# Low parts of the first 18 weight tiles on VectorE inside the attention loop, the later ones on GpSimd in four pieces

## The chip, the cores and the metric

The kernel runs on one core of one Trainium2 chip. The metric is the device time of one execution in microseconds (us). Engines: TensorE (PE), VectorE (DVE), ScalarE (ACT), GpSimd (POOL) and SyncE (SP, which issues the loads).

## The reference

A causal decoder trunk of two layers over 512 tokens of width 1024, in float32, followed by a final RMSNorm:

```python
for layer in range(2):
    h = rms_norm(x, mix_norm_g[layer])
    y = even_mixer(h, ...) if layer == 0 else odd_mixer(h, ...)
    x = x + y
    x = x + conv_ffn(rms_norm(x, ffn_norm_g[layer]), ...)
return rms_norm(x, final_norm_g)
```

The even mixer has one input projection (1024 x 3072), rotary positions, four differential attention heads (A: two 64-wide maps and a 128-wide value each) and eight dilated heads of 64 (B), then an output projection. The odd mixer has multi-head latent attention (C, four heads) beside stick-breaking attention (D, four heads of 128), and an output projection. The MLP is `(silu(conv3(gate)) * value) @ w_down` with 2816 channels.

## The kernel before

**Three products for one.** The large matrix products are made from split operands. An operand `a` is rounded to a shorter format (`hi`), and the rest is `lo = a - hi`. TensorE then sums `h_hi*w_hi + h_hi*w_lo + h_lo*w_hi` (PASSES, L1064).

**Weight tiles.** All weights are cut into 101 tiles of 128 x 2048 float32 (1 MB), taken in a fixed order through two slots: tile n is in slot n % 2. For each tile, SyncE loads `w_raw` (L258), ScalarE rounds it to `w_hi` (split_hi, L356), GpSimd subtracts to get `w_lo` (split_lo, L276, one instruction over 2048 columns), and TensorE multiplies. The counters `w_hi_ready`, `w_lo_ready` and `mm_done` order this. SyncE loads tile n+2 only once `w_lo_ready` has counted tile n, since both hi and lo are made from the raw tile.

**Order in time.** Every engine has its own program, written out by hand, and they meet only at semaphores.

- Prologue, 0 to about 57 us: the first norm, token tile by token tile (square on ScalarE, L681 to L684 and L717 on VectorE, transposes on TensorE at L1072, high parts on ScalarE, low parts on VectorE at L699), woven with the projection of head group 0 from tiles 0 and 1 (L1371). VectorE copies the sums (L760) and does the rotary embedding of token tiles 2 and 3 itself (`rope`, L944 to L947); GpSimd does tiles 0 and 1 (rope_tile, L303 to L306).
- Head groups 0 to 6, in two loops (A: g = 0 to 3, B: g = 4 to 6), each with nine or ten steps k. At step k TensorE makes the scores of unit k (L1260 to L1264), then a part of the projection of the next group g+1 (part, L1226: parts 0 to 3 from tile 2g+2, parts 4 to 7 from tile 2g+3), the transposes of unit k-1 (L1287), and the value product of unit k-2 (L1305). VectorE makes the row maximum (L802), in B groups the multiplication with the dilation counts (L808, whose result the transposes wait for), the division of finished outputs (L815 to L826), and copies or adds each part (L767, L770). GpSimd, in its own loop, subtracts tile 2g+2, does the rotary embedding of the four token tiles as their parts come, and subtracts tile 2g+3. When all four are done TensorE transposes them (turn_qk, L1215) and the next group begins.
- Between A and B, VectorE makes the norm factors of the A outputs (L670, L690 to L692) and scales them (L974).
- Group 7 (B) has no next group. In its place the first half of the output projection is turned (L1171) and multiplied (L1191). The rest of the output projection follows (L1110), then the norm before the MLP.
- MLP (up and gate L1125 and L1154, down L1341), the odd layer's projections, D with the latent projections (L1429, L1452, L1466; VectorE scans at L1010), C, output projection, MLP, final norm. In the down product VectorE makes the low parts of the activations (L892) from SBUF.

GpSimd works its splits in these later parts one tile after the other as `w_hi_ready` counts up, in `split_range`.

Of the kernel before, what the change touches and what calls it, by code (L numbers as in the profile page):

```python
# [23 lines left out]
FT = DFF // 128  # L24
UNIT = 2048
EPS = 1e-6
LAM_INIT = 0.8 - 0.6 * math.exp(-0.3 * 0)
# [24 lines left out]
def trunk_program(nc, x_in, weights, consts, masks, vectors, gains, out):  # L52
# [5 lines left out]
    with ExitStack() as ctx:  # L58
# [212 lines left out]
        def _(pool):  # L271
            own = Own(pool, pool_own)

            def split_lo(m, slot):
                pool.wait_ge(w_hi_ready, m + 1)
                pool.tensor_tensor(w_lo[:, slot, :], w_raw[:, slot, :], w_hi[:, slot, :].bitcast(f32),  # L276
                                   ALU.subtract).then_inc(w_lo_ready, 1)

# [28 lines left out]

            split_lo(0, 0)
            split_lo(1, 1)
            pool.wait_ge(cst_loaded, 16)  # L310
            for t in range(2):
                rope_tile(0, t, 2 * t + 2)
            split_lo(2, 0)
            split_lo(3, 1)
            with pool.Fori(1, 8) as g:
                end = own.loop(g - 1, 7, 12)
                pool.wait_ge(qk_turned, 2 * g)
                split_lo(2 * g + 2, 0)
                for t in range(NT):
                    pool.wait_ge(rope_ready, 4 * g + t - 1)  # L320
                    rope_tile(g, t)
                split_lo(2 * g + 3, 1)
                end()
            split_range(W_OUT0 + 2, W_UKV + 1)

# [336 lines left out]
        def _(ve):  # L662
# [23 lines left out]
            def refine(a, b):  # L686
# [5 lines left out]
                own.link(ve.scalar_tensor_tensor(rstd[:, cols], rs_a[:, cols], 1.5, sd[:, cols], ALU.add, ALU.mult))  # L692

            def lows(b):

# [24 lines left out]
            def tile_lows(t):  # L720
                lows(2 * t)
                lows(2 * t + 1)
# [69 lines left out]
            def attention(kind, h, g, ahead=False, between=None):  # L792
# [5 lines left out]
                for k in range(11):  # L798
# [43 lines left out]
                    if ahead:  # L842
                        for u in FILL.get(k, ()):
                            copy_part(g + 1, u, 4 + u % 2)
                        if k == 9:
                            copy_k(g + 1)

            def late_first(n, t):
# [63 lines left out]
            ve.wait_ge(gain_loaded, 16)  # L912
            scale_x(0, 0, xn)
            tile_lows(0)
            tile_variance(0, 1)
            rsqrt(1, 2)
            scale_x(0, 1, xn)
            tile_variance(0, 2)
            tile_lows(1)
# [37 lines left out]
            own.mark(ve.tensor_scalar(sub_gain[:, :], vec[:, V_SUB:V_SUB + 128], 1.0 - LAM_INIT, None, ALU.mult))  # L957
            copy_k(0)
            ve.wait_ge(lam_exps, 1)
            own.link(ve.tensor_tensor(neg_lam[:, :], lam_s[:, 3:4], lam_s[:, 2:3], ALU.subtract))  # L960
# [660 lines left out]
```

## Time and profile before

Three runs: 1376.17, 1376.79 and 1376.96 us, median 1376.79. The profiled execution has a span of 1375.9 us from its first to its last instruction; so about 0.9 us of the median lies around the span.

| | |
|---|---|
| PE busy | 1283.3 us, 93% |
| DVE / ACT / POOL busy | 575.6 / 472.1 / 542.0 us |
| TensorE's granted clock, mean | 0.975 |
| POOL L276, split of a weight tile, 128x2048 | x101, mean 4605 ns |
| POOL L303 / L304 / L305 / L306, one rotary tile | mean 773 / 464 / 457 / 761 ns |
| DVE L808, 128x128 / x256 / x384 / x512 | mean 1164 / 1944 / 614 / 1243 ns |
| DVE L817, 128x1 | x16, mean 1261 ns |
| DVE L802, 128x256 / L767, 128x384 | mean 425 / 557 ns |
| DVE L944, 128x256, at 53.73 us | 0.43 us |
| ACT L356, high part of a weight tile | x101, mean 1912 ns |
| DVE L1010, 128x384, at 851.28 us | 0.96 us |
| DVE L717, 128x1024, two inputs in SBUF | x16, mean 1295 ns |

How to read it: a busy share is an average over stages with different limits. A mean duration of an instruction includes time that it was held up after it had begun; where a small shape has a larger mean than a big one (L808), some of its instances were held.

### The profile page before, as it was taken

The page shows a single profiled execution, that of the slowest core. Times are in us where ns is not written, and L with a number is a line of the kernel's source. Part 1 is how long each engine was busy: PE and PEld are TensorE (multiplying, and loading weights), DVE is VectorE, ACT ScalarE, POOL GpSimd, SP SyncE. Part 2 cuts the span into 40 slices and gives each one's busy share as a digit, 9 for nine tenths or more (in the row PEclk, how much of TensorE's full clock was granted, in tenths as well). Part 3 has the DMA queues.
Part 4 walks back from the last instruction along what each step waited for, and adds up shares of the span by engine and source line. Part 5 has one row for each costly group of instructions (what it writes and reads, how often), then busy time and mean ns, then how long its engine had stood idle before and what let it go on. Part 6 is the DMA issues. An engine that isn't in the chain of part 4 may idle for free.

```text
span 1375.9 us, 17106 instructions
## 1 busy us (share of the span) xinstructions
PE 1283.3 (93%) x6340; PEld 1072.5 (78%) x6344; DVE 575.6 (42%) x885; ACT 472.1 (34%) x646; POOL 542.0 (39%) x234
## 2 busy tenths in 40 slices
PE   3699988888999999999999998689999999999997
PEld 3688877776788888888887887577888888888885
DVE  5555665554451221215456215844442121225554
ACT  3233423323252332224333225534343222334332
POOL 3355545442244444444443442331144444444441
PEclk9899999999999999999999999899999999999999
DMA  6211110110122222232222321111032223222221
GB/s 239 77 62 61 61 62 32 60 61 31 61 91 109 91 91 91 91 111 103 92 92 73 126 92 62 61 36 57 31 108 91 91 92 120 93 92 92 91 92 61
DMA packets 17032, 114.69 MB, mean 83 GB/s; under 512 B 1888, under 2 KB 2016, under 8 KB 4064
## 3 DMA queue, kind: packets, MB, share of 16 engines
q1 hardware_dynamic: 16128, 110.99, 22.4%
q10 hardware_dynamic: 864, 3.15, 0.7%
q8 instruction: 28, 0.46, 0.1%
q14 instruction: 12, 0.10, 0.0%
HBM read 112.03 MB, written 2.10 MB: 83 GB/s over the span
## 4 chain that ended last, share of the span: by engine, by line
PE 50%; issue 32%; POOL 8%; DVE 6%; ACT 2%; DMA 0%; POOLq 0%; DVEq 0%; ACTq 0%
PE ps L1154 17%; PE ps L1226 8%; POOL w_lo L276 7%; PE ps L1341 7%; PE ps L1260 4%; PE ps L1305 2%; PE ps L1429 2%; PE ps L1110 2%; PE ps L1191 2%; PE ps L1371 1%; PE ps L1287 1%; PE ps L1466 1%; PE ps L1125 1%; PE ps L1452 1%; PE ps L1072 1%
## 5 line engine op out<-in xcount | busy, mean ns | idle before, releaser
L276 POOL TENSOR_TENSOR w_lo<-w_raw,w_hi 128x2048 fp32r<-128x2048 f32 x101 | 465.0, 4605 | 731.9 <-ACT w_hi L356 731.9
L356 ACT ACTIVATE w_hi<-w_raw 128x2048 fp32r<-128x2048 f32 x101 | 193.1, 1912 | 377.6 <-PE ps L1154 177.3
L1154 PE MATMUL ps<-hT_hi,w_hi 128*128 128x512 f32 x720 | 280.1, 389 | 0.0
L1154 PE MATMUL ps<-hT_hi,w_lo 128*128 128x512 f32 x720 | 280.1, 389 | 0.0
L1154 PE MATMUL ps<-hT_lo,w_hi 128*128 128x512 f32 x720 | 280.1, 389 | 0.0
L1154 PEld LDWEIGHTS ps<-hT_lo,w_hi 128*128 128x128 f32 x720 | 135.2, 188 | 28.2
L1154 PEld LDWEIGHTS ps<-hT_hi,w_hi 128*128 128x128 f32 x720 | 135.2, 188 | 27.9
L1154 PEld LDWEIGHTS ps<-hT_hi,w_lo 128*128 128x128 f32 x720 | 135.2, 188 | 27.8
L892 DVE TENSOR_TENSOR hT_lo<-region,hT_hi 128x2048 fp32r<-128x2048 f32 (+1 forms) x22 | 100.6, 4579 | 106.5 <-ACT hT_hi L528 106.5
L862 DVE SCALAR_TENSOR_TENSOR qk<-ps,vec,qk 128x511 f32<-128x511 f32 x44 | 33.0, 750 | 202.9 <-ACT qk L502 202.9
L1341 PE MATMUL ps<-w_hi,hT_hi 128*128 128x512 f32 x256 | 99.6, 389 | 0.0
L1341 PE MATMUL ps<-w_lo,hT_hi 128*128 128x512 f32 x256 | 99.6, 389 | 0.0
L1341 PE MATMUL ps<-w_hi,hT_lo 128*128 128x512 f32 x256 | 99.6, 389 | 0.0
L502 ACT ACTIVATE qk<-ps,vec 128x512 f32<-128x512 f32 x44 | 34.3, 780 | 178.4 <-PE ps L1154 166.3
L872 DVE TENSOR_TENSOR region<-ps,qk 128x512 f32 (+1 forms) x44 | 30.4, 691 | 153.4 <-PE ps L1154 153.4
L1226 PE MATMUL ps<-w_hi,hT_hi 128*128 128x384 f32 x224 | 84.6, 378 | 0.0
L1226 PE MATMUL ps<-w_lo,hT_hi 128*128 128x384 f32 x224 | 78.2, 349 | 0.0
L1226 PE MATMUL ps<-w_hi,hT_lo 128*128 128x384 f32 x224 | 78.1, 349 | 0.0
L1260 PE MATMUL ps<-qk 64*128 64x128 f32 (+7 forms) x160 | 66.2, 495 | 1.3 <-DVE qk L755 0.9
L487 ACT ACTIVATE xn<-ps 128x128 f32<-128x128 f32 (+3 forms) x80 | 34.8, 435 | 92.3 <-PE ps L1287 92.3
L802 DVE TENSOR_REDUCE neg_max<-ps 128x1 f32<-128x128 f32 (+3 forms) x80 | 39.2, 490 | 49.7 <-PE ps L1262 24.7
L1305 PE MATMUL ps<-region,xn 128*128 (+2 forms) x400 | 57.3, 275 | 0.5 <-ACT xn L487 0.5
(195 smaller groups left out, 2081.4 us busy)
## 6 DMA issues: line engine op xcount, KB each, us to landing
w_raw<-weights SPq DMA_DIRECT2D x101, 1024.0 KB, 4.8
gain<-gains ACTq DMA_DIRECT2D x5, 512.0 KB, 3.7
out<-region SPq DMA_DIRECT2D x4, 512.0 KB, 2.6
x<-x_in SPq DMA_DIRECT2D x3, 512.0 KB, 10.8
cst<-consts SPq DMA_DIRECT2D x1, 640.0 KB, 12.6
x<-x_in ACTq DMA_DIRECT2D x1, 512.0 KB, 6.5
region<-masks SPq DMA_DIRECT2D x1, 384.0 KB, 13.3
vec<-vectors SPq DMA_DIRECT2D x1, 282.5 KB, 12.8
```

The lines of the kernel that those rows point to most:

```text
L276: pool.tensor_tensor(w_lo[:, slot, :], w_raw[:, slot, :], w_hi[:, slot, :].bitcast(f32), ALU.subtract).then_inc(w_lo_ready, 1)
L356: sc.activation(w_hi[:, slot, :], w_raw[:, slot, :], ACT.Copy).then_inc(w_hi_ready, 1)
L487: sc.activation(probsT[:, m, 0:w], ps[:, 2 + m, 0:w], ACT.Copy).then_inc(pT_copied, 1)
L502: sc.activation(qk[:, s, :], ps[:, s, :], ACT.Identity, scale=vec[:, ds(8 * i + (col + 2), 1)], bias=vec[:, ds(8 * i + (col + 3), 1)]).the ...
L802: ve.tensor_reduce(neg_max[:, k:k + 1], ps[:, m, 0:w], AX.X, ALU.max, negate=True)\
L862: own.link(ve.scalar_tensor_tensor(qk[:, s, 1:SEQ], ps[:, s, 0:SEQ - 1], vec[:, ds(8 * i + (col + 1), 1)], qk[:, s, 1:SEQ], ALU.mult, ALU. ...
L892: ve.tensor_tensor(hT_lo[:, places, :], act[:, ds(kt, count), :], hT_hi[:, places, :].bitcast(f32), ALU.subtract).then_inc(act_lo[l], count)
L1154: ins = pe.matmul(bank, w[:, slot, k * pitch + 128 * s:k * pitch + 128 * s + 128], h[:, k:k + 1, :], start=k == 0 and n == 0, stop=k == KT ...
L1226: ins = pe.matmul(ps[:, bank, 0:384], h_[:, 4 * half + k, t * 128:(t + 1) * 128], w_[:, half, k * 384:(k + 1) * 384], start=k == 0 and n = ...
L1260: pe.matmul(ps[:, m, 0:w], q, kk, start=True, stop=False)
L1305: ins = pe.matmul(o, probsT[:, m, b * 128:(b + 1) * 128], v, start=b == 0, stop=b == i)
L1341: ins = pe.matmul(ps[:, 4 * c + t, :], a[:, t * 128:(t + 1) * 128], w[:, slot, u * 512:(u + 1) * 512], start=first and u == units[0] and n ...
```

## The change

VectorE gets its own `split_lo`, the same subtraction as one instruction over 2048 columns. It is called three times ahead of the loops (tiles 0, 1 and 2), and in each group's steps after the copy of a part: after step 1 for tile 2g+3 and, where there is a next group, after step 6 for tile 2g+4. That makes tiles 3 to 17. GpSimd keeps only its rotary tiles in these stages. It waits until `w_lo_ready` has counted 18 tiles and then goes on with tile 18, each tile now in four instructions of 512 columns with the semaphore on the last.

```diff
--- before.py
+++ after.py
@@ -23,6 +23,7 @@
 KT = DM // 128
 FT = DFF // 128
 UNIT = 2048
+LO_COLS = 512
 EPS = 1e-6
 LAM_INIT = 0.8 - 0.6 * math.exp(-0.3 * 0)
 
@@ -272,9 +273,13 @@
             own = Own(pool, pool_own)
 
             def split_lo(m, slot):
+
                 pool.wait_ge(w_hi_ready, m + 1)
-                pool.tensor_tensor(w_lo[:, slot, :], w_raw[:, slot, :], w_hi[:, slot, :].bitcast(f32),
-                                   ALU.subtract).then_inc(w_lo_ready, 1)
+                for c in range(0, UNIT, LO_COLS):
+                    cols = slice(c, c + LO_COLS)
+                    ins = pool.tensor_tensor(w_lo[:, slot, cols], w_raw[:, slot, cols],
+                                             w_hi[:, slot, cols].bitcast(f32), ALU.subtract)
+                ins.then_inc(w_lo_ready, 1)
 
             def split_range(a, b):
                 b = min(b, n_tiles)
@@ -305,22 +310,17 @@
                 own.link(pool.tensor_tensor(t2[:, :, 32:64], src[:, :, 0:32], sin[:, :, 32:64], ALU.mult))
                 pool.tensor_tensor(dst, t1, t2, ALU.add).then_inc(rope_ready, 1)
 
-            split_lo(0, 0)
-            split_lo(1, 1)
             pool.wait_ge(cst_loaded, 16)
             for t in range(2):
                 rope_tile(0, t, 2 * t + 2)
-            split_lo(2, 0)
-            split_lo(3, 1)
             with pool.Fori(1, 8) as g:
                 end = own.loop(g - 1, 7, 12)
                 pool.wait_ge(qk_turned, 2 * g)
-                split_lo(2 * g + 2, 0)
                 for t in range(NT):
                     pool.wait_ge(rope_ready, 4 * g + t - 1)
                     rope_tile(g, t)
-                split_lo(2 * g + 3, 1)
                 end()
+            pool.wait_ge(w_lo_ready, W_OUT0 + 2)
             split_range(W_OUT0 + 2, W_UKV + 1)
 
             pool.wait_ge(c_copied, 8)
@@ -690,6 +690,12 @@
                 own.link(ve.tensor_tensor(rs_a[:, cols], sd[:, cols], sd[:, cols], ALU.mult))
                 own.link(ve.scalar_tensor_tensor(rs_a[:, cols], rs_a[:, cols], -0.5, var[:, cols], ALU.mult, ALU.mult))
                 own.link(ve.scalar_tensor_tensor(rstd[:, cols], rs_a[:, cols], 1.5, sd[:, cols], ALU.add, ALU.mult))
+
+            def split_lo(m, slot):
+
+                ve.wait_ge(w_hi_ready, m + 1)
+                ve.tensor_tensor(w_lo[:, slot, :], w_raw[:, slot, :], w_hi[:, slot, :].bitcast(f32),
+                                 ALU.subtract).then_inc(w_lo_ready, 1)
 
             def lows(b):
 
@@ -844,6 +850,11 @@
                             copy_part(g + 1, u, 4 + u % 2)
                         if k == 9:
                             copy_k(g + 1)
+                    if g_static is None or g_static == 7:
+                        if k == 1:
+                            split_lo(2 * g + 3, 1)
+                        if k == 6 and ahead:
+                            split_lo(2 * g + 4, 0)
 
             def late_first(n, t):
 
@@ -911,10 +922,12 @@
             rsqrt(0, 1)
             ve.wait_ge(gain_loaded, 16)
             scale_x(0, 0, xn)
+            split_lo(0, 0)
             tile_lows(0)
             tile_variance(0, 1)
             rsqrt(1, 2)
             scale_x(0, 1, xn)
+            split_lo(1, 1)
             tile_variance(0, 2)
             tile_lows(1)
             rsqrt(2, 3)
@@ -956,6 +969,7 @@
               .then_inc(lam_dots, 1)
             own.mark(ve.tensor_scalar(sub_gain[:, :], vec[:, V_SUB:V_SUB + 128], 1.0 - LAM_INIT, None, ALU.mult))
             copy_k(0)
+            split_lo(2, 0)
             ve.wait_ge(lam_exps, 1)
             own.link(ve.tensor_tensor(neg_lam[:, :], lam_s[:, 3:4], lam_s[:, 2:3], ALU.subtract))
             own.link(ve.tensor_scalar(neg_lam[:, :], neg_lam[:, :], -LAM_INIT, None, ALU.add))
```

## Rows read from the trace of the kernel before

**Rows 1.** The page: busy time, share of the span and instructions of each engine.
```profile
PE 1283.3 (93%) x6340; PEld 1072.5 (78%) x6344; DVE 575.6 (42%) x885; ACT 472.1 (34%) x646; POOL 542.0 (39%) x234
```

**Rows 2.** Busy time by stretch: each engine (instructions), TensorE's granted clock, DMA share, GB/s.
```profile
0.00:57.00 57.00, 25.92 (x136) 24.56 (x136) 34.76 (x51) 19.60 (x27) 24.22 (x16) 0.93 0.51 191
...
189.00:234.00 45.00, 37.19 (x191) 30.61 (x191) 25.92 (x59) 12.42 (x22) 18.58 (x18) 0.89 0.13 48
...
234.00:314.00 80.00, 71.03 (x372) 58.95 (x374) 42.45 (x89) 22.56 (x39) 37.06 (x36) 0.91 0.15 52
```

**Rows 3.** Chain that ended last, prologue: start us, us, what.
```profile
10.75 2.92 DVE rs_a L682
...
13.69 4.43 DVE rs_a L683
...
43.98 4.02 DVE xn L944
...
47.99 4.50 DVE xn L945
```

**Rows 4.** Timeline of VectorE, prologue: start us, us, engine, line, what.
```profile
24.03 0.16 DVE L682 TENSOR_TENSOR rs_a<-rstd 128x1 f32<-128x1 f32 x1
...
54.07 0.28 DVE L945 TENSOR_TENSOR xn<-region,cst 128x128 f32<-128x128 f32 x1
```

**Rows 5.** Chain that ended last, end of the second A group.
```profile
122.25 0.74 POOL stage L306
```

**Rows 6.** Timeline of VectorE, from A to B, and B groups (brackets: idle before).
```profile
190.77 4.24 DVE L670 TENSOR_SCALAR var<-ss 128x16 f32<-128x16 f32 x1 [0.21 <-DVE o_tmp L822]
...
237.11 2.67 DVE L808 SCALAR_TENSOR_TENSOR xn<-xn,cst 128x128 f32<-128x128 f32 x1
...
248.76 4.49 DVE L808 SCALAR_TENSOR_TENSOR xn<-xn,cst 128x256 f32<-128x256 f32 x1 [0.34 <-ACT xn L473]
...
348.56 5.04 DVE L808 SCALAR_TENSOR_TENSOR xn<-xn,cst 128x512 f32<-128x512 f32 x1
```

**Rows 7.** Timeline of TensorE in the B groups; brackets: idle before it, releaser.
```profile
198.43 0.33 PE L1287 MATMUL ps<-cst,xn 128*128 128x128 f32 x1 [4.11 <-DVE xn L808]
...
239.84 0.33 PE L1287 MATMUL ps<-cst,xn 128*128 128x128 f32 x1 [0.81 <-DVE xn L808]
...
253.31 0.63 PE L1287 MATMUL ps<-cst,xn 128*128 128x128 f32 x2 [3.40 <-DVE xn L808]
...
353.66 0.66 PE L1287 MATMUL ps<-cst,xn 128*128 128x128 f32 x4 [1.87 <-DVE xn L808]
```

**Rows 8.** Chain that ended last, one B group, on TensorE.
```profile
240.17 0.63 PE ps L1260 x2
...
256.70 3.77 PE ps L1226 x12
...
266.96 2.10 PE ps L1226 x12
```

**Rows 9.** Groups of GpSimd's instructions by line and form.
```profile
L342 POOL TENSOR_TENSOR region<-region,cst 128x512 f32<-128x512 f32 x1 | 1.3, 1293 | 15.7 <-DVE region L1024 15.7
```

**Rows 10.** Timeline of GpSimd, first gated MLP.
```profile
427.12 4.61 POOL L276 TENSOR_TENSOR w_lo<-w_raw,w_hi 128x2048 fp32r<-128x2048 f32 x1 [7.09 <-ACT w_hi L356]
...
633.02 4.61 POOL L276 TENSOR_TENSOR w_lo<-w_raw,w_hi 128x2048 fp32r<-128x2048 f32 x1 [5.59 <-ACT w_hi L356]
```

**Rows 11.** Timeline of VectorE, first MLP and stick-breaking attention.
```profile
435.30 0.69 DVE L872 TENSOR_TENSOR region<-ps,qk 128x512 f32 x1 [4.75 <-PE ps L1154]
...
634.85 4.93 DVE L892 TENSOR_TENSOR hT_lo<-region,hT_hi 128x2048 fp32r<-128x2048 f32 x1 [3.06 <-ACT hT_hi L528]
...
880.96 3.22 DVE L1010 TENSOR_TENSOR_SCAN stage<-stage 128x384 f32<-128x384 f32 x1
...
884.69 3.81 DVE L690 TENSOR_TENSOR rs_a<-sd 128x8 f32<-128x8 f32 x1
```

**Rows 12.** Timeline of TensorE, first tile after the norm.
```profile
388.33 0.39 PE L1125 MATMUL ps<-hT_hi,w_hi 128*128 128x256 f32 x1 [0.74 <-POOL w_lo L276]
```

## The prediction

> **What bounds the kernel now.** I read the page first: TensorE is busy for 1283.3 us of the 1375.9 us span [rows 1]. So nearly all that can be won lies in the 93 us in which TensorE stands still, and in the stretches where it runs at its lower clock. The busy time by stretch says where: TensorE works for 25.92 of the first 57 us, and in the B groups its mean granted clock is 0.89 and 0.91 of full speed, where the mean of the whole is 0.975 [rows 2]. The chain of waits names the holder in the prologue: tiny VectorE instructions, one column wide, last 2.92 and 4.43 us, and two rotary instructions 4.02 and 4.50 us [rows 3], where the same lines take 0.16 and 0.28 us elsewhere [rows 4]. All of them read two operands in SBUF while GpSimd subtracts a weight tile (4.6 us each, L276), and they end when its instruction ends. Instructions that read PSUM show nothing of the kind. The same happens from A to B (4.24 us for sixteen columns) and in the B groups at L808, which lasts 2.67 to 5.04 us where a 128x384 takes 0.61 (mean in the table) [rows 6]. Behind these TensorE stands idle for 4.11, 0.81, 3.40 and 1.87 us [rows 7]. So it is a lock between VectorE and GpSimd that is held for a whole instruction. The change takes the long GpSimd instructions out of these stages and cuts the later ones in four.
>
> The Trainium skill says the same in "SBUF — State Buffer", section "Who interferes with whom": the pair of ports is locked for the whole instruction and the second to come blocks fully, whichever it is. That speaks against the change in one way: VectorE's own splits now block GpSimd's rotary instructions. The trace here shows clearly only the other direction, GpSimd holding VectorE. If the lock held in that direction alone, the rotary terms below (4 x 0.25 and 3 x 1.0 us) would fall away and the time would be 4 us less, 1335; by the rule it is the sum below.
>
> **What a split costs on VectorE.** L892 is the same operation with the same shape. It starts at 634.85 us and lasts 4.93, beside a GpSimd split that ends at 633.02 + 4.61 = 637.63 [rows 10, 11]. What is left after that is 639.78 - 637.63 = 2.15 us. L717 has 1024 columns in 1.295 us (table); twice that is 2.6, the upper end. I take 2.2 us. There are 18.
>
> **Prologue: -13.6 us.** Gone: 2.92 + 4.43 - 2 x 0.16 = 7.0 us ahead of the first transposes, and 4.02 + 4.50 less 0.43 and 0.28 for what the two take (the second rotary tile's L944, in the table, and L945) = 7.8 us ahead of turn_qk [rows 3, 4]. Added: split 0 stands behind the first scale_x, beside the transposes and ScalarE's copy, which take about as long, so nothing is left of it. Split 1 (2.2 us) stands after the second scale_x and must be over before TensorE has done 12 projection matmuls and 8 transposes, some 5.5 us: hidden. Split 2 stands right behind copy_k(0), and TensorE needs it after one pair of score matmuls, some 1.1 us: it costs 2.2 - 1.1 = 1.1 us. Sum -7.0 - 7.8 + 1.1 = -13.7, with 0.1 for semaphores -13.6. Bounds: -9 (the next late thing, such as a load of x, takes 4 to 5 of it) and -16 (TensorE, idle for some 4 instead of 10 us before turn_qk, keeps its clock).
>
> **A groups: +1 us.** They are bound by TensorE. VectorE's stalls there (L817) already lie beside parts, so taking them away gives nothing. At the end of each group TensorE waits for the last rotary tile, which ends at 122.99 in the group that began near 92 [rows 5]. Split 2g+4 begins when part 6 is copied, exactly when rotary tile 2 could start; it holds GpSimd for 2.2 us, the tile then takes 2.4 (sum of the table's four), and the last tile's data are there 4.4 us after part 6 (one step: two scores, part, transposes). So GpSimd is late by 2.2 + 2.4 - 4.4 = 0.2 to 0.3 us per group, four times. Bounds 0 and 1 us per group.
>
> **B groups: -23.4 us.** Gone in each: the idle 0.81 and 3.40 us [rows 7] with some 0.3 lost around them (TensorE's own end to the idle time), 4.5 us. Then the clock: after the 3.40 us TensorE runs at the lower of its two levels (1.2 instead of 2.4 GHz); part L1226 takes 3.77 us and not 2.10 [rows 8], and with the score, mask, transpose and value matmuls beside it I count 3.3 us. Together 7.8. Added: after step 1 the copy, the split, the maximum (0.43) and the multiplication (0.28) take 0.56 + 2.2 + 0.7 = 3.5 us with overlaps, ahead of which TensorE has one score (0.63 and mask 0.22) and one part (2.10) [rows 8], 3.1: +0.4. After step 6, a score of 1.05, its mask, a part and transposes cover 4.3 us of VectorE's work, so no stall; but GpSimd's rotary tiles 2 and 3 now alternate with the split and two multiplications of 0.7: +1.0. Net -6.4 for g = 5 and 6. For g = 4 there is no first short stall, but the 4.24 us from A to B go, which are 4.11 of idle TensorE [rows 6, 7] and by the same count some 1.7 of low clock behind it: 5.8, with 6.5 for the second stall and its clock 12.3. Added are 1.4, and 0.3 since VectorE is still late from the norm factors: -10.6. Sum 10.6 + 2 x 6.4 = 23.4. Bounds: -10 (the six splits on the chain in full, 6 x 2.2 = 13 more) and -28 (nothing added).
>
> **Group 7 and what follows: -2.0 us.** The split at group 7's start now sits on VectorE ahead of a multiplication: +0.45. At its end L808 waits for a piece instead of a tile, 1.3 us [rows 9] instead of 4.3, and TensorE's idle 1.87 us [rows 7] goes: -1.9. Later a split on GpSimd takes four pieces of 1.29 us [rows 9], overlapping by 0.04: 5.05 instead of 4.61, +0.45. Where TensorE waits for w_lo itself, this counts: first tile after three norms (wait 0.74 [rows 12]), partly taken up by the next wait, 3 x 0.35; the first latent tile, where a scan also gets in between, +0.85. At the end of each down product L892 now gets in after two pieces and the last two follow it, 637.63 + 0.45 + 2.2 by analogy, so w_lo comes last: 2 x 0.45. In D the held instructions, 3.22 and 3.81 us, shrink [rows 11]. But L690 to L692 are three in a row and each may wait for a piece of its own, up to 1.3 us, so of the 3.81 only 1.0 is saved; of the scan's 3.22 (0.96 when free, table) 1.6, and of the scans beside an earlier split 0.7 (estimate, half a piece): -3.3. Sum +0.45 - 1.9 + 1.05 + 0.85 + 0.9 - 3.3 = -2.0. Bounds: +3 (nothing saved in D, where each new wait meets a piece) and -5 (3.65 of L690 saved too, and the norms' waits absorbed).
>
> **MLPs: 0.** The pieces are free while TensorE doesn't want the tile: w_lo is done at 431.73, and the pair it belongs to starts when L872's part ends, 435.2 [rows 10, 11], 3.5 us of cover against 0.45. In the down product the split may end 0.45 + 2.2 later, still inside one tile's 10.9 us with 1.9 (ScalarE's high part) + 5.05 + 2.2 = 9.2.
>
> **Sum.** -13.6 + 1.0 - 23.4 - 2.0 = -38.0 against the profiled span of 1375.9: span 1337.9, and with the 0.9 us around it **1338.8 us**.
>
> **Rivals.**
>
> *VectorE becomes the holder.* Each of the 15 splits in the groups (tiles 3 to 17) lands on the chain with its full 2.2 us, since L808 and L802 stand behind it in order: 15 x 2.2 = 33 against the 6.0 that I added for them (4 x 0.25, 3 x 1.4, 0.3, 0.45): time 1376.8 - 38 + 27 = 1366. For it: at step 1 the cover is already 0.4 short. Against: at step 6 and in all A groups it is there in the rows.
>
> *The clock does not come back.* The stalls go but TensorE still falls to 1.2 GHz in the B groups and in the prologue: less by 3 x 3.3 + 1.7 = 11.6: 1350. For it: short waits remain. Against: the part two steps later runs at 2.10 again [rows 8], so TensorE recovers as soon as it is busy.
>
> *Pieces starve (slower).* A GpSimd instruction may have a price of its own that the 512-column rows do not show with four in a row, or VectorE gets in between each two. Place: the 66 MLP tiles. It decides from a piece of 2.0 us on ((4.6 + 3.5)/4); at 2.2 us each tile is 0.7 us late: 66 x 0.7 = 46 us, time 1376.8 - 38 + 46 = 1385. Against it stands 1.29 for such a shape [rows 9], and L862 to L872 read PSUM and hold nothing.
>
> *More is won*, as the prologue and all B groups run at full clock with rotary tiles hidden: 1331.
>
> **Chances.** Forecast with its own range 1333 to 1345: 0.62. VectorE the holder 0.14, clock 0.10, more won 0.10, pieces starve 0.04. The range that should hold 8 in 10 is 1328 to 1356: it leaves out most of the first rival and the slower one. This kernel's runs tell 0.2% (2.8 us) from no change: faster 0.95, same 0.01, slower 0.04.
>
> **What would show it.** Right: in the prologue L682 and L683 at 0.16 us, turn_qk near 40 us; every L808 under 1 us but for waits behind rotary instructions; granted clock near 1 in the B groups, and a B group of about 34 us where it is 40; VectorE's split at 2.2 to 2.4 us; L892 between 2.2 and 3.5. Wrong: TensorE waiting more than 1 us behind step 1's multiplication in each B group, rotary tile 3 over 1.5 us later than its part, or a first matmul of an MLP tile that waits for w_lo.

## The result, and the profile after

The changed kernel takes 1334.78 us (median of 4 runs, 1334.67 to 1336.24) against 1376.88 (4 runs, 1376.17 to 1378.09) for the kernel before beside it: ratio 0.9694, interval 0.968 to 0.9708. The forecast was 1338.8. The profiled execution has a span of 1333.0 us against 1375.9, so 42.9 us are gone where the sum had 38.0.

The page of the changed kernel, busy time, then the windows of its trace (us; busy time of each engine with its instructions; TensorE's granted clock; DMA share; GB/s) over the prologue, groups 3 to 4, 5 and 6, and most of group 7:

```profile
PE 1268.5 (95%) x6340; PEld 1061.6 (80%) x6344; DVE 508.8 (38%) x903; ACT 471.9 (35%) x646; POOL 559.2 (42%) x465
```

```profile
0.00:42.00 42.00, 25.32 (x136) 24.11 (x136) 24.53 (x54) 19.97 (x27) 6.05 (x12) 1.00 0.55 209
175.00:209.20 34.20, 32.77 (x187) 27.20 (x188) 22.71 (x61) 12.14 (x21) 12.63 (x17) 1.00 0.18 63
209.20:277.60 68.40, 65.67 (x380) 54.95 (x381) 39.86 (x95) 23.33 (x39) 25.17 (x33) 1.00 0.17 61
277.60:312.00 34.40, 29.90 (x144) 21.75 (x144) 16.30 (x39) 12.39 (x22) 0.00 (x0) 0.95 0.09 31
```

VectorE does 18 subtractions more and is busy for 67 us less [rows 1]. With 2.28 us for each of the 18, some 108 of its 575.6 busy us had been time held up inside an instruction (an estimate: 66.8 + 18 x 2.28). TensorE's granted clock in the B groups is 1.00 where it was 0.89 and 0.91 [rows 2]. The prologue, in the chain of the changed kernel (`...` stands for rows left out):

```profile
10.79 0.17 DVE rs_a L682
10.98 0.17 DVE rs_a L683
...
12.65 2.20 DVE w_lo L697
...
39.23 0.42 DVE xn L957
39.66 0.20 DVE xn L958
...
44.71 4.21 PE ps L1240 x12
```

The four long instructions of [rows 3] are short (L957 and L958 are L944 and L945 of before). The last row is the first part of the next group's projection, behind 1.12 us of waiting for tile 2. It runs at the lower of TensorE's two levels, as it did in the kernel before, where the same twelve matmuls stand in the chain like this:

```profile
58.96 3.72 PE ps L1226 x12
```

What TensorE waited for from 175 us to the end of group 7 (line, releaser: us in total, times, longest), changed kernel first, then the kernel before over the same stages (there 189 to 364 us):

```profile
PE ps L1301 <- DVE xn L814: 7.2, 7, 3.5
```

```profile
PE ps L1287 <- DVE xn L808: 21.1, 12, 4.1
```

Where the 42.9 us went, stage by stage. A group is measured from one copy_k to the next, in us. The stretch called D runs from the first matmul of the latent projections (L1429 before) to the first one behind the query product (L1466 before). TensorE's wait at the latent tile is inside it, so its forecast of +0.85 stands there:

| stage | before | after | difference | forecast |
|---|---|---|---|---|
| to copy_k(0) | 57.14 | 41.77 | -15.4 | |
| group 0 | 34.13 | 36.15 | +2.0 | -13.6 with the line above; +0.25 for the group |
| groups 1 to 3, each | 32.23 | 32.56 | +0.33 | +0.25 |
| group 4 | 44.72 | 34.14 | -10.6 | -10.6 |
| groups 5 and 6, each | 40.3 | 33.92 | -6.4 | -6.4 |
| group 7, to the output product's late half | 50.33 | 47.54 | -2.8 | -1.45 |
| from there to D | 459.25 | 459.58 | +0.3 | +1.15 |
| D | 83.47 | 78.55 | -4.9 | -2.45 |
| the rest | 469.5 | 469.7 | +0.2 | +0.8 |

### The profile page after: what moved, and what is told of

Its sections match the earlier page's. It is cut to its first block, busy times and chain, and to the rows that moved or that the text cites. A ratio compares the mean times of both kernels' runs of the same rounds, so it can differ in the third digit from the quotient of the medians.

```text
span 1333.0 us, 17355 instructions
## 1 busy us (share of the span) xinstructions
PE 1268.5 (95%) x6340; PEld 1061.6 (80%) x6344; DVE 508.8 (38%) x903; ACT 471.9 (35%) x646; POOL 559.2 (42%) x465
## 4 chain that ended last, share of the span: by engine, by line
issue 42%; POOL 32%; PE 20%; DVE 4%; ACT 2%; POOLq 1%; DMA 0%; DVEq 0%; ACTq 0%
POOL w_lo L280 30%; PE ps L1240 9%; PE ps L1274 3%; PE ps L1443 2%; PE ps L1385 1%; PE ps L1319 1%; PE ps L1301 1%; DVE w_lo L697 1%; PE ps L1466 1%; POOL tmp L308 0%; DMA w_raw<-weights 0%; ACT w_hi L356 0%; ACT tmp L399 0%; PE ps L1495 0%; POOL stage L311 0%
## 5 line engine op out<-in xcount | busy, mean ns | idle before, releaser
L280 POOL TENSOR_TENSOR w_lo<-w_raw,w_hi 128x512 fp32r<-128x512 f32 x332 | 465.0, 1431 | 551.1 <-ACT w_hi L356 551.1
L308 POOL TENSOR_TENSOR tmp<-region,cst 128x256 f32<-128x256 f32 x30 | 36.8, 1225 | 186.7 <-DVE region L776 158.4
L903 DVE TENSOR_TENSOR hT_lo<-region,hT_hi 128x2048 fp32r<-128x2048 f32 (+1 forms) x22 | 58.9, 2685 | 144.0 <-ACT hT_hi L528 144.0
L1240 PE MATMUL ps<-w_hi,hT_hi 128*128 128x384 f32 x224 | 81.6, 364 | 1.1 <-DVE w_lo L697 1.1
L1274 PE MATMUL ps<-qk 64*128 64x128 f32 (+7 forms) x160 | 63.2, 476 | 1.3 <-DVE qk L761 0.9
## 6 DMA issues: line engine op xcount, KB each, us to landing
region<-masks SPq DMA_DIRECT2D x1, 384.0 KB, 13.3
vec<-vectors SPq DMA_DIRECT2D x1, 282.5 KB, 12.8
```

The costliest lines, as they stand in the source:

```text
L280: ins = pool.tensor_tensor(w_lo[:, slot, cols], w_raw[:, slot, cols], w_hi[:, slot, cols].bitcast(f32), ALU.subtract)
L308: own.mark(pool.tensor_tensor(t1, src, cos, ALU.mult))
L903: ve.tensor_tensor(hT_lo[:, places, :], act[:, ds(kt, count), :], hT_hi[:, places, :].bitcast(f32), ALU.subtract).then_inc(act_lo[l], count)
L1240: ins = pe.matmul(ps[:, bank, 0:384], h_[:, 4 * half + k, t * 128:(t + 1) * 128], w_[:, half, k * 384:(k + 1) * 384], start=k == 0 and n = ...
L1274: pe.matmul(ps[:, m, 0:w], q, kk, start=True, stop=False)
```

## The experiments

Twelve kernels ran. I tell them in three sets: which part does what, where the splits stand, and how long the pieces are. The lengths of the groups and the time from group 7's start to the end of the span ("rest") are from the traces. In e3, groups 5 and 6 took 40.3 and 38.8 us. In the diffs `...` stands for lines left out, and the comments are not in the kernels.

| kernel | to copy_k(0) | group 0 | 1 to 3, each | 4 | 5, 6, each | rest |
|---|---|---|---|---|---|---|
| before | 57.14 | 34.13 | 32.23 | 44.72 | 40.3 | 1062.6 |
| after | 41.77 | 36.15 | 32.56 | 34.14 | 33.92 | 1055.4 |
| e1 | 41.68 | 36.18 | 32.57 | 34.15 | 33.92 | 1061.6 |
| e2 | 52.74 | 34.41 | 32.19 | 38.39 | 33.22 | 1054.0 |
| e3 | 41.83 | 36.16 | 32.19 | 45.44 | 39.5 | 1064.3 |
| e4 | 53.13 | 35.27 | 32.57 | 33.79 | 33.77 | 1056.4 |
| e5 | 41.49 | 35.21 | 32.23 | 38.39 | 33.22 | 1055.8 |
| e6 | 41.45 | 35.29 | 32.18 | 33.93 | 33.21 | 1054.1 |
| e7 | 41.51 | 35.57 | 32.21 | 33.31 | 32.83 | 1056.2 |
| e9 | 41.96 | 36.29 | 32.21 | 33.31 | 32.83 | 1053.7 |

### Which part does what

**e1: later tiles whole.** VectorE's splits stay; GpSimd's are whole again.

```diff
-LO_COLS = 512
+LO_COLS = 2048
```

> The changed kernel with GpSimd's later splits as one instruction of 2048 columns again; the first 18 tiles stay on VectorE. Theory (a lock held for one whole instruction): group 7's last multiplication is held about 4.3 us again instead of 1.1, +2.2; the scans and L690 in D are held 2 to 4 us again, +4.9 with the low clock behind; less 0.4 per place where TensorE waits for w_lo. About 1341 us. Rival (dividing is worth nothing, all the gain is VectorE's speed and the moved work): 1333 to 1335, as each split is 0.4 us shorter.

Measured: 1341.88 us (1340.89 to 1342.6), ratio 0.9742 (0.9726 to 0.9758). The groups are the same to 0.1 us; the 6 us are all behind group 7's start: 3.6 at that group's end (47.5 to 51.1) and 3.1 in D (78.6 to 81.6), of which 0.5 comes back in the other stretches.

**e2: pieces alone.** The kernel before, each GpSimd split in four pieces, at its old place; nothing on VectorE.

```diff
+LO_COLS = 512
...
-                pool.tensor_tensor(w_lo[:, slot, :], w_raw[:, slot, :], w_hi[:, slot, :].bitcast(f32),
-                                   ALU.subtract).then_inc(w_lo_ready, 1)
+                for c in range(0, UNIT, LO_COLS):
+                    cols = slice(c, c + LO_COLS)
+                    ins = pool.tensor_tensor(w_lo[:, slot, cols], w_raw[:, slot, cols],
+                                             w_hi[:, slot, cols].bitcast(f32), ALU.subtract)
+                ins.then_inc(w_lo_ready, 1)
```

> The kernel before with one edit: GpSimd's splits in four pieces of 512 columns, all still on GpSimd. Theory (the lock is held for one instruction, so a waiting VectorE instruction gets in after at most 1.3 us): B groups lose their long stalls, L808 under 2 us, -7 us each; the prologue only -3, because there each of several VectorE instructions in a row pays a piece; later stages -7 as in the changed kernel. About 1344 us. Rival (the move to VectorE is what counts): only the later 7 us, about 1370.

Measured: 1344.09 us (1342.94 to 1344.44), ratio 0.9753 (0.9737 to 0.977). So the pieces alone bring 33.3 of the 42.9 us of span. Group 4 keeps 4 us of the loss, and this is what its VectorE looks like when the sixteen factors of the normalisation are made (timeline: start, us, engine, line, operation; in brackets idle time before):

```profile
186.52 0.95 DVE L674 TENSOR_SCALAR var<-ss 128x16 f32<-128x16 f32 x1 [0.21 <-DVE o_tmp L826]
188.00 0.71 DVE L694 TENSOR_TENSOR rs_a<-sd 128x16 f32<-128x16 f32 x1 [0.53 <-ACT sd L393]
188.75 1.20 DVE L695 SCALAR_TENSOR_TENSOR rs_a<-rs_a,var 128x16 f32<-128x16 f32 x1
189.99 1.19 DVE L696 SCALAR_TENSOR_TENSOR rstd<-rs_a,sd 128x16 f32<-128x16 f32 x1
```

GpSimd's four pieces run from 186.09 to 191.14. Each of VectorE's short instructions ends with a piece and pays for one; behind them TensorE stands idle for 3.4 us.

**e3: prologue alone.** The kernel before, tiles 0 to 2 on VectorE, whole tiles on GpSimd for the rest. GpSimd's tile 3 now waits until tile 2 is counted.

```diff
-            split_lo(0, 0)          # GpSimd
-            split_lo(1, 1)
...
-            split_lo(2, 0)
+            pool.wait_ge(w_lo_ready, 3)
             split_lo(3, 1)
...
             scale_x(0, 0, xn)
+            split_lo(0, 0)          # VectorE, as in the change; 1 and 2 too
...
```

> The kernel before with tiles 0, 1 and 2 on VectorE; all other splits on GpSimd, undivided. Theory: the prologue is 13.4 us shorter (15.4 at copy_k(0), less 2.0 in the first group, which waits for tile 2), nothing else changes: 1363.5. Rival (gains overlap, the time reappears in the groups): 1368 or more.

Measured: 1364.73 us (1364.14 to 1365.28), ratio 0.9904 (0.9888 to 0.9921). Prologue and group 0 together are 13.3 us shorter.

**e4: the rest without the prologue.** The changed kernel with tiles 0 to 2 back on GpSimd, whole.

```diff
+            split_whole(0, 0)       # GpSimd
+            split_whole(1, 1)
...
+            split_whole(2, 0)
...
             scale_x(0, 0, xn)
-            split_lo(0, 0)          # VectorE
```

> The changed kernel with tiles 0, 1 and 2 on GpSimd, undivided, as before. Theory: the prologue is as long as before and everything else as in the changed kernel: 1334.8 + 13.4 = 1348.2; with e3 the two parts add up to the whole. Rival (they overlap): 1340 or less.

Measured: 1344.03 us (1342.63 to 1345.62), ratio 0.9752 (0.9736 to 0.9769), 4 us less than expected. I had taken the whole prologue as belonging to tiles 0 to 2. Its chain shows which term was not theirs:

```profile
44.27 4.02 DVE xn L963
48.28 0.20 DVE xn L964
```

The second of the two rotary instructions, 4.50 us before [rows 3], was held by the split of tile 3. That tile is one of the later ones, and it is gone here. In e3 it isn't gone, but it now comes after tile 2 and so after the rotary instructions. This is why the spans gained by e3 and e4, 12.5 and 32.1 us, add up to more than the 42.9 of the change.

### Where the splits stand

**e5: GpSimd in the loop.** e3 with pieces on GpSimd: VectorE has tiles 0 to 2 only, and GpSimd all from tile 3 on at the old places. The diff is against the changed kernel.

```diff
-                    if g_static is None or g_static == 7:     # VectorE, attention loop
-                        if k == 1:
-                            split_lo(2 * g + 3, 1)
-                        if k == 6 and ahead:
-                            split_lo(2 * g + 4, 0)
...
+            pool.wait_ge(w_lo_ready, 3)                       # GpSimd
+            split_lo(3, 1)
...
                 pool.wait_ge(qk_turned, 2 * g)
+                split_lo(2 * g + 2, 0)
                 for t in range(NT):
                     pool.wait_ge(rope_ready, 4 * g + t - 1)
                     rope_tile(g, t)
+                split_lo(2 * g + 3, 1)
```

> Here VectorE subtracts only tiles 0 to 2; every tile from 3 on is subtracted by GpSimd in four pieces, at the places of the kernel before. It asks what the VectorE subtractions inside the attention loop are worth once the pieces are there. Theory A (pieces and prologue do all; from the lengths of the groups in the runs so far: the prologue and first group as with tiles 0 to 2 on VectorE, 41.8 + 36.2; three groups of 32.2 as with pieces alone; group 4 38.4, groups 5 and 6 33.2 each; 1054.0 from there to the end): span 1333.4, median about 1335, that is, the same as the changed kernel (1334.8). Theory B (the loop's subtractions on VectorE carry a part of their own, as my sum had it with 10.6 and 6.4 us per group won by them): 1355 or more.

Measured: 1336.0 us (1334.43 to 1337.27), ratio 0.9704 (0.9691 to 0.9717); the changed kernel's is 0.9694 (0.968 to 0.9708). Once the pieces are there, the VectorE splits in the loop bring nothing that can be measured. By the groups they win 4.3 us in group 4 and lose 0.33 in each A group, 0.7 in each of groups 5 and 6, and 1.9 us in group 7; groups 1 to 7 together come out even. Prologue and group 0 are 1.2 us shorter in e5, the stretches from group 7's end on 2.3 us longer. Most of that is the clock in D (see below).

**e6: after the norm.** e5, and GpSimd starts tile 11 when the normalised output of the first four heads is there (first tile).

```diff
                     rope_tile(g, t)
+                if after_norm:                                # group 4 alone
+                    pool.wait_ge(src_ready, 5)
                 split_lo(2 * g + 3, 1)
```

> As e5, but GpSimd subtracts tile 11 only after the normalisation of the first four heads' output, so that none of its pieces stands beside those VectorE instructions. Theory A (in group 4 the only thing wrong with pieces on GpSimd is that each instruction of the normalisation pays a piece): group 4 falls from 38.4 to about 33.5 us, span 1328.5, median 1330, 4 to 5 us under the changed kernel. Rival (tile 11 then comes too late for step 4 of group 4, or the long group has another reason): no better than e5, 1335 or above.

Measured: 1330.62 us (1328.87 to 1330.93), ratio 0.9661 (0.9648 to 0.9674). The same line as above, and GpSimd's split, which now starts at 178.62:

```profile
176.07 0.18 DVE L682 TENSOR_SCALAR var<-ss 128x16 f32<-128x16 f32 x1 [0.21 <-DVE o_tmp L840]
```

```profile
178.62 5.09 POOL L279 TENSOR_TENSOR w_lo<-w_raw,w_hi 128x512 fp32r<-128x512 f32 x4 [5.88 <-DVE region L995]
```

0.18 in place of 0.95 us, and group 4 falls from 38.39 to 33.93. This version is 4 us faster than the changed kernel (intervals 0.9648 to 0.9674 and 0.968 to 0.9708). The split did not have to leave GpSimd; it had to wait.

**e7: moved splits.** The changed kernel; VectorE's first split of a turn stands before the copy in step 1, the second in step 4.

```diff
+                        if k == 1:
+                            split_lo(2 * g + 3, 1)
                         for u in FILL.get(k, ()):
                             copy_part(g + 1, u, 4 + u % 2)
...
-                    if g_static is None or g_static == 7:
-                        if k == 1:
-                            split_lo(2 * g + 3, 1)
-                        if k == 6 and ahead:
-                            split_lo(2 * g + 4, 0)
+                    if g_static == 7 and k == 1:
+                        split_lo(2 * g + 3, 1)
+                    if k == 4 and ahead:
+                        split_lo(2 * g + 4, 0)
```

> The changed kernel with VectorE's two subtractions of a loop turn at other places: the first ahead of the copy of the part in step 1, the second in step 4 in place of step 6. Theory A (what the groups lose, 32.57 us against 32.19 and 33.92 against 33.22 with GpSimd's pieces, is the 2.29 us for which VectorE's later instructions of that step wait, and it depends on where they stand): 0.3 x 4 + 0.6 x 3 = 3 us less than the changed kernel, about 1331.8. Rival (VectorE's busy time itself is what counts, wherever it stands): 1334.8, no change; if step 4 is a worse place, up to 1337.

Measured: 1330.82 us (1329.65 to 1331.78), ratio 0.9666 (0.9653 to 0.9679). The A groups lose what they had paid (32.56 to 32.21 us, and 32.23 in the kernel before). Groups 5 and 6 lose 1.1 each (33.92 to 32.83), which is more than the 0.7 by which they were behind e5. In the changed kernel the price of a place shows on TensorE in step 1 of group 5, on GpSimd in step 6 of an A group, and on TensorE at that group's end (three timelines of the changed kernel):

```profile
219.72 0.33 PE L1301 MATMUL ps<-cst,xn 128*128 128x128 f32 x1 [0.59 <-DVE xn L814]
```

```profile
103.40 2.62 POOL L308 TENSOR_TENSOR tmp<-region,cst 128x256 f32<-128x256 f32 x1 [2.27 <-DVE region L776]
```

```profile
110.03 0.44 PE L1229 MATMUL ps<-cst,stage 128*128 128x128 f32 x2 [0.46 <-POOL stage L311]
```

L308 takes 0.73 us when free; here VectorE's split (103.14 to 105.43) holds it for 1.9 us. So GpSimd is held by VectorE too. This is what the Trainium skill has in "SBUF — State Buffer", section "Who interferes with whom": the second to come is blocked, whichever it is.

**e9: moved splits, and tile 17 on GpSimd.** The diff is against e7.

```diff
-                    if g_static == 7 and k == 1:              # VectorE
-                        split_lo(2 * g + 3, 1)
...
-            pool.wait_ge(w_lo_ready, W_OUT0 + 2)
-            split_range(W_OUT0 + 2, W_UKV + 1)
+            pool.wait_ge(w_lo_ready, W_OUT0 + 1)
+            split_range(W_OUT0 + 1, W_UKV + 1)
```

> The kernel of e7 (VectorE's subtractions of the loop moved to the start of step 1 and to step 4), and tile 17 is subtracted by GpSimd in pieces instead of by VectorE in step 1 of group 7. Theory A (from the last turn of the loop to the first matmul of the output product it was 48.2 us in e7 and 45.7 us in e6, where GpSimd has tile 17; VectorE's 2.29 us stand in the path there): 1330.8 - 2.5 = 1328.3, a version that beats both kernels. Rival (the 2.5 us come from something else that e6 changed, as when its tile 16 was ready): 1330.8, no change against e7.

Measured: 1329.42 us (1329.23 to 1332.03), ratio 0.9659 (0.9645 to 0.9672). The median is 1.4 us under e7's, within what the two spread; in the traces the time from group 7's start to the first matmul of the output product's late half falls from 48.2 to 45.6 us, as expected. But 0.7 of these 2.6 us is the clock and not the split: with the same split and the same 3.48 us of standing, group 7 takes 47.5 us at a mean granted clock of 0.96 in the changed kernel and 48.2 at 0.93 in e7. Prologue and group 0 happened to take 1.2 us more than in e7, so the span is 1.3 us shorter.

**e10: tile 63 late.** The changed kernel; in D, GpSimd waits with tile 63 until the latent's low parts are made.

```diff
-            split_range(W_OUT0 + 2, W_UKV + 1)
+            split_range(W_OUT0 + 2, W_UKV)
+            pool.wait_ge(c_lo, 5)
+            split_lo(W_UKV, W_UKV % 2)
```

> The changed kernel; GpSimd subtracts tile 63 (the one after tile 62 in the decay attention) only when the latent's low parts are made, so that none of its pieces stands beside the three instructions of the inverse root and the scan that follows. Theory A (while the refinement waits, ScalarE's rounding of tile 63, 843.35 to 845.25, and its three steps to 846.9 hold the attention's path as late as VectorE's refinement does, so that only the scan at 849.97, 1.46 against 0.69 us, is on the path): 0.8 us less than the changed kernel, 1334.0. Rival (VectorE's refinement holds the path: a piece at each of its last two instructions goes as well): 3 us less, 1331.8.

Measured: 1333.06 us (1332.38 to 1333.76), ratio 0.9678 (0.9664 to 0.9691), span 1331.2, 1.8 us less than the changed kernel's: between the two expectations. TensorE's waits in D, changed kernel first, then e10:

```profile
PE ps L1519 <- DVE xn L1053: 6.3, 2, 5.1
...
PE ps L1466 <- DVE hT_lo L1060: 1.6, 1, 1.6
```

```profile
PE ps L1521 <- DVE xn L1055: 5.2, 2, 4.1
...
PE ps L1468 <- DVE hT_lo L1062: 0.7, 1, 0.7
```

Both places gave 0.9 to 1.0, and D as a whole is 1.5 us shorter (78.55 to 77.03). The three-instruction refinement of the norm factors (L690 to L692) did hold the path, for about one of its pieces; I had put that at nothing.

**e12: the three together.** e9 with tile 63 late.

> The kernel of e9 with tile 63 late as in e10. Theory (the two edits stand in different stages and each takes pieces away from other VectorE instructions, so they add): span 1327.6 - 1.8 = 1325.8, median about 1327.6, 7 us under the changed kernel. Rival (the time that e10 won is given back by what waits for GpSimd next, once the phase against the loads has shifted): 1329.4, no change against e9.

Measured: 1327.1 us (1324.39 to 1327.77), ratio 0.9632 (0.9619 to 0.9645), span 1325.3. The edits add, and this version beats both kernels: 7.7 us under the changed one, with intervals apart (0.9619 to 0.9645 against 0.968 to 0.9708).

### How long the pieces are

**e8 and e11: 1024 and 256 columns.**

```diff
-LO_COLS = 512
+LO_COLS = 1024                  # e8; in e11 256
```

> The changed kernel with two pieces of 1024 columns per GpSimd subtraction in place of four of 512. Theory A (a VectorE instruction that meets a piece waits for its end, so the price goes with the length of a piece): whole tiles (4.61 us) cost 7.1 us more than 512 columns (1.29 us); a piece of 1024, estimated at 2.4 us, costs 7.1 x (2.4 - 1.3) / 3.3 = 2.4 us more: about 1337. Rival (waits of under some 2.5 us are hidden beside TensorE's work): 1334.8, no change.

> The changed kernel with eight pieces of 256 columns in place of four of 512. Theory A (price by the length of a piece, 3.2 us for 1024 columns and 7.1 us for 2048 over 512, some 2.1 to 2.9 us of time for each us of piece; a piece of 256 estimated at 0.7 us, 0.6 us less): 1.3 to 1.7 us less, about 1333.3. Rival (an instruction that waits lets through one piece whatever its length, and a tile's last piece comes later: eight pieces take about 5.7 us in place of 5.05 and the places where TensorE waits for the last piece pay it): 1334.8 to 1337.

Measured: e8 1337.99 us (1337.02 to 1339.13), ratio 0.9719 (0.9706 to 0.9733); e11 1337.22 us (1334.89 to 1339.28), ratio 0.9707 (0.9693 to 0.972), span 1335.6 in both.

e8's time came as its theory had it, but not for its reason. Group 7 takes 47.6 us, as with 512 columns, and D takes 81.8, as with whole tiles (81.6 in e1). The theory had the price in proportion to the piece. The row of three dependent instructions in D shows why it isn't:

```profile
844.33 1.66 DVE L690 TENSOR_TENSOR rs_a<-sd 128x8 f32<-128x8 f32 x1
846.02 2.27 DVE L691 SCALAR_TENSOR_TENSOR rs_a<-rs_a,var 128x8 f32<-128x8 f32 x1
848.33 2.27 DVE L692 SCALAR_TENSOR_TENSOR rstd<-rs_a,sd 128x8 f32<-128x8 f32 x1
```

That is 6.2 us, where whole tiles cost the row 3.81 + 0.38 + 0.24 = 4.4 (kernel before, and e1). Two tiles, 62 and 63, stand one behind the other here. Whole, the first holds the scan ahead of the row and the second holds L690. In halves each instruction of the row meets a piece. With the scan (1.05 against 3.22 us) it is 7.3 against 7.7 us: halves win next to nothing.

e11's span is 2.6 us longer than with 512 columns. The duration of a GpSimd piece is about 4607, 2395, 1292 and 737 ns for 2048, 1024, 512 and 256 columns, so a tile as a whole takes longer with each division. What TensorE waited for from group 7 on shows both sides, first whole tiles (e1), then 512 columns, then 256:

```profile
PE ps L1519 <- DVE xn L1053: 12.8, 3, 8.6
...
PE ps L1139 <- POOL w_lo L280: 1.9, 3, 0.8
```

```profile
PE ps L1519 <- DVE xn L1053: 8.5, 3, 5.1
...
PE ps L1139 <- POOL w_lo L280: 3.1, 3, 1.2
...
PE ps L1124 <- POOL w_lo L280: 2.0, 2, 1.0
```

```profile
PE ps L1519 <- DVE xn L1053: 7.6, 3, 4.5
PE ps L1139 <- POOL w_lo L280: 4.8, 3, 1.7
...
PE ps L1124 <- POOL w_lo L280: 3.1, 2, 1.6
```

The waits for held VectorE instructions fall from 12.8 to 8.5 to 7.6; those for the last piece of a tile rise from 1.9 to 5.1 to 7.9 (and at the first latent tile from 0.8 to 1.5 to 1.9). In e1 TensorE waited at L1124 too, 1.6 us for L903, so at the same places it is 3.5, 5.1 and 7.9.

Not all of e11's 2.6 us is the pieces'. In group 7 it takes 49.0 us against 47.5 with the same waits. The lower level lasts longer there, before any piece has begun: the granted clock is 0.93 over the group, and 0.96 in the changed kernel. The stretches behind group 7 are 1.9 us longer, which the waits above explain. The medians differ by 2.4 us with overlapping intervals (0.9693 to 0.972 and 0.968 to 0.9708). So 512 columns is the best of the four by the waits; that it beats 256 in time is likely, not shown.

## Why the prediction was right, and where it was off

**The mechanism** holds: the short instructions are short, the clock is back in the B groups, and the stalls behind L808 went from 21.1 to 7.2 us, of which 3.5 are at VectorE's own split in group 7.

**The split on VectorE** is 2.28 us (2.2 taken); the row of its place in group 5:

```profile
216.84 2.28 DVE L697 TENSOR_TENSOR w_lo<-w_raw,w_hi 128x2048 fp32r<-128x2048 f32 x1
```

**Prologue, A and B groups**: -36.0 forecast, -35.75 measured, and close in every line of the table. copy_k(0) came 15.4 us earlier where the held instructions gave 14.8; turn_qk ran at the higher level of the clock, 1.08 us (40.67, L1229) instead of 1.95 (55.16, L1215), which I had only in the bound of -16. Group 0 then pays 2.0 us: the 1.12 us wait that I had priced at 1.1, 0.5 because the first part runs at the lower level to its end (4.21 us against 3.72), and 0.33 as the other A groups. Of what I gave to tiles 0 to 2, some 4 us were tile 3's (e4).

**The branch that said 1335.** The prediction also worked out 1335 for a lock that holds VectorE alone, and 1334.78 was measured. That the numbers agree is luck: GpSimd is held too (L308, 2.62 us, in e7's rows), and the A groups pay for it, 0.33 us each. The 4 us between forecast and result are group 7 and D.

**What the prediction had not asked**: whether the tiles had to go to VectorE at all. It wrote the 23.4 us of the B groups to the splits' leaving GpSimd. e2 and e5 show that pieces at the old place bring all of it but 4.3 us in group 4, and e6 gets those by a wait. The forecast of the time is untouched by this, since the long GpSimd instruction is gone from these groups either way.

**Group 7**: two terms mis-sized, against each other. VectorE's split at its start was put at +0.45. In e6, where GpSimd has tile 17, this group takes 45.6 us against 47.5, so the split costs 1.9. The stand behind it, changed kernel:

```profile
287.14 0.33 PE L1301 MATMUL ps<-cst,xn 128*128 128x128 f32 x1 [3.48 <-DVE xn L814]
```

The end was put at -1.9; with pieces and no VectorE split (e6) the group is 4.7 us under 50.33. The kernel before had three stalls there, not one, 4.6 us in all, and the lower clock behind them (0.93 over the group, 0.96 in e6).

```profile
PE ps L1287 <- DVE xn L808: 4.6, 3, 2.0
```

**D, -4.9 instead of -2.45.** VectorE's rows are as forecast, three in a row that pay a piece each (changed kernel):

```profile
844.20 0.58 DVE L690 TENSOR_TENSOR rs_a<-sd 128x8 f32<-128x8 f32 x1
844.82 1.19 DVE L691 SCALAR_TENSOR_TENSOR rs_a<-rs_a,var 128x8 f32<-128x8 f32 x1
...
846.04 1.19 DVE L692 SCALAR_TENSOR_TENSOR rstd<-rs_a,sd 128x8 f32<-128x8 f32 x1
```

TensorE's longest stand there was 8.6 us before (L1505) and is 5.1 now, -3.5, and an earlier one behind a scan went from 3.0 to 2.2, -0.8; against them stands 0.9 more ahead of the query product. That is -3.4, about the -3.3 that I forecast, and the latent tile's +0.6 against +0.85 is too. What is missing is the product itself: its 36 matmuls take 7.9 instead of 9.7 us, since the first of them ran at the lower level before, 0.52 us each, and at the higher one after. (Some 0.3 us of the -4.9 are left over.) First the kernel before, then the changed one:

```profile
894.55 0.66 PE L1452 MATMUL ps<-w_hi,hT_hi 128*128 128x384 f32 x1 [0.69 <-DVE hT_lo L1046]
895.00 0.52 PE L1452 MATMUL ps<-w_lo,hT_hi 128*128 128x384 f32 x1
```

```profile
853.16 0.41 PE L1466 MATMUL ps<-w_hi,hT_hi 128*128 128x384 f32 x1 [1.58 <-DVE hT_lo L1060]
853.41 0.33 PE L1466 MATMUL ps<-w_lo,hT_hi 128*128 128x384 f32 x1
```

It would be easy to say that the shorter stand gave the clock back to the product. The experiments don't bear that out for this product. e6 has the same short stand and the slow first matmuls; e1 has the long stand and the fast ones (the stand and the product's first matmul, e6 and then e1):

```profile
840.95 2.08 PE L1526 MATMUL ps<-region,xn 128*128 128x128 f32 x8 [5.12 <-DVE xn L1060]
...
846.09 0.66 PE L1473 MATMUL ps<-w_hi,hT_hi 128*128 128x384 f32 x1 [1.26 <-DVE hT_lo L1067]
```

```profile
854.97 2.07 PE L1519 MATMUL ps<-region,xn 128*128 128x128 f32 x8 [8.61 <-DVE xn L1053]
...
859.55 0.41 PE L1466 MATMUL ps<-w_hi,hT_hi 128*128 128x384 f32 x1 [1.08 <-DVE hT_lo L1060]
```

In all four the matmuls right behind the stand run at 1.2 GHz; whether the clock is back before the query product or within it differs, and what decides that I have not settled.

The product alone misleads, though. Over the whole of D, e6 takes 78.7 us, no more than the changed kernel's 78.6, because it kept the higher level in an earlier stretch. The six kernels that are alike here (the changed one, e2, e4, e6, e7, e9) lie within 78.5 to 78.7 us at a granted clock of 0.93. e5, alike too, takes 80.6 at 0.92, and that is 2.1 of the 2.3 us by which it is behind the changed kernel after group 7. With the long stand it is 81.6 in e1 at 0.92, and 83.5 and 83.9 in the kernel before and e3 at 0.90. So of the -4.9 us the pieces show 3.1 (against e1); the other 1.8 is a lower level that lasted longer in the kernel before, and its cause stays open.

**Norms, first latent tile, ends of the down products**: +2.8 forecast, +1.2 measured (0.3 and 0.2 in the table, and 0.6 at the latent tile: 1.5 us of waiting instead of 0.9). TensorE does wait longer for w_lo, 3.1 instead of 1.9 us behind the three norms, as forecast (+1.05). But the norms' own VectorE instructions are held for less, and TensorE's wait for them (L1086, L1072 before) falls from 1.6 to 0.4 us. The prediction had put that at nothing. At the ends of the down products it waited 1.6 us for L892 before and waits 2.0 for w_lo now, +0.4 instead of +0.9. L903 (L892 before) gets in between pieces as forecast:

```profile
596.38 2.87 DVE L903 TENSOR_TENSOR hT_lo<-region,hT_hi 128x2048 fp32r<-128x2048 f32 x1 [3.06 <-ACT hT_hi L528]
```

```profile
594.55 7.10 POOL L280 TENSOR_TENSOR w_lo<-w_raw,w_hi 128x512 fp32r<-128x512 f32 x4 [3.19 <-ACT w_hi L356]
```

Only the last tile of a down product pays for the 7.10 us.

**The rivals.** VectorE as the holder (1366), the clock that stays low (1350) and starving pieces (1385) are out. The reason given against the second was too strong: in the kernel before TensorE was busy through the whole part of 3.77 us [rows 8] and still ran at the lower level. What the first says does exist, but at 1.9 us in group 7 and 0.3 to 1.1 in a group. The last one, *more is won* (1331), asked for hidden rotary tiles. The change doesn't hide them; e7 does, and takes 1330.8.

## What to carry to other kernels

When one engine's short instructions are as long as another's long ones, cut the long one first, and hold it back where a row of short dependent instructions stands; move it to the other engine last, since there it holds both queues. Cut until what the last piece costs its consumer outweighs what the held instructions win: here at about a quarter of a tile. Count the dependent instructions in a row first: a row of three was held for longer by halves of tiles than by whole ones (e8). A stage with TensorE at rest in it can come out 1 to 2 us apart in kernels that are alike there (e5 in D, e7 and e11 in group 7): read the stage's granted clock before explaining it.

## What the runs showed of the hardware that I had not expected

- A row of dependent VectorE instructions, eight or sixteen columns wide, pays up to one piece each (1.19 to 1.20 us at 512 columns). The three in D take 4.4 us beside whole tiles, 6.2 beside halves (e8), 3.0 beside quarters and 2.0 beside eighths (e11). Free, one takes 0.17 (e10), so about 0.5 for three.
- Per column GpSimd's pieces are dearer the smaller they are: from the first to the end of the last, 2048 columns take 4.61 us in one, 4.74 in two, 5.04 in four and 5.6 in eight, where nothing is in their way.
- VectorE does the same 2048 columns in 2.28 us, half of GpSimd's time, and still the loop was no faster for it (e5).
